# Gate and up projections of a decoder step's feed-forward as seven block products in place of eight, in two passes of 544 tokens

## The reference

```python
def merge_and_ffn(x, conv_out, attn_out, w_out, ffn_norm_g, w_gate, w_up, w_down):
    mix = jnp.concatenate([conv_out, attn_out.astype(conv_out.dtype)], axis=-1)
    x = x + jnp.einsum('bte,ed->btd', mix, w_out)
    h = rms_norm(x, ffn_norm_g)
    f = jax.nn.silu(jnp.einsum('btd,df->btf', h, w_gate)) * jnp.einsum('btd,df->btf', h, w_up)
    return x + jnp.einsum('btf,fd->btd', f, w_down)
```

## Time and profile before

| | us |
|---|---|
| median of 3 runs | 1621.68 |
| lowest, highest run | 1618.64, 1622.87 |
| profiled execution | 1625.65 |
| its span, first to last instruction | 1623.9 |
| PE, DVE, ACT, POOL busy | 1525.2, 888.5, 428.1, 550.8 |
| mean granted PE clock, as a share of 2.4 GHz | 0.973 |

### The profile page before, as it was taken

One profiled execution on the slowest core, in us unless ns is written; L12 is line 12 of the kernel. 1 busy time (PEld: TensorE's weight loads), 2 busy tenths in 40 slices (PEclk: granted clock), 3 DMA queues, 4 the chain that ended last, 5 costly groups with the idle time before them and its releaser, 6 DMA issues.

```text
span 1623.9 us, 24357 instructions
## 1 busy us (share of the span) xinstructions
PE 1525.2 (94%) x9069; PEld 1400.5 (86%) x9069; DVE 888.5 (55%) x1568; ACT 428.1 (26%) x788; POOL 550.8 (34%) x436
## 2 busy tenths in 40 slices
PE   4999988889968888899999999999999999999999
PEld 4998777538846767799989999999999999999999
DVE  7799989999867874444353241423324241433323
ACT  4100258755265554452140101010000101010010
POOL 4543211041258800115333425343342534333320
PEclk9999999989978998899999999999999999999999
DMA  6312100120163331232101101111111111111103
GB/s 209 85 48 73 58 13 25 28 79 7 50 216 118 111 96 42 65 136 80 40 26 52 53 26 55 48 39 50 41 41 37 52 38 52 39 52 39 39 0 110
DMA packets 68638, 100.17 MB, mean 62 GB/s; under 512 B 12017, under 2 KB 49137, under 8 KB 68431
## 3 DMA queue, kind: packets, MB, share of 16 engines
q1 hardware_dynamic: 63714, 94.32, 18.0%
q10 hardware_dynamic: 4853, 4.93, 0.9%
HBM read 86.57 MB, written 13.02 MB: 61 GB/s over the span
## 4 chain that ended last, share of the span: by engine, by line
PE 73%; DVE 13%; issue 6%; ACT 5%; DMA 1%; POOL 1%; ACTq 0%; DVEq 0%; POOLq 0%
PE ps L942 21%; PE ps L944 21%; PE ps L943 21%; DVE mcnt L2193 2%; PE ps L1261 2%; PE ps L1249 1%; ACT rl L1644 1%; PE ps L1233 1%; DVE y L2072 1%; PE ps L1234 1%; PE ps L1346 1%; DVE acc L2134 1%; ACT sm L1791 1%; PE ps L1390 1%; PE ps L1303 1%
## 5 line engine op out<-in xcount | busy, mean ns | idle before, releaser
L942 PE MATMUL ps<-hi_t,w_hi 128*128 128x384 f32 (+2 forms) x1464 | 479.1, 327 | 2.4 <-DVE lo_t L2535 2.4
L944 PE MATMUL ps<-hi_t,w_lo 128*128 128x384 f32 (+2 forms) x1464 | 478.0, 326 | 0.0
L943 PE MATMUL ps<-lo_t,w_hi 128*128 128x384 f32 (+2 forms) x1464 | 477.7, 326 | 0.0
L942 PEld LDWEIGHTS ps<-hi_t,w_hi 128*128 128x128 f32 (+1 forms) x1464 | 274.2, 187 | 3.9 <-issue 1.6
L943 PEld LDWEIGHTS ps<-lo_t,w_hi 128*128 128x128 f32 (+1 forms) x1464 | 274.2, 187 | 0.6
L944 PEld LDWEIGHTS ps<-hi_t,w_lo 128*128 128x128 f32 (+1 forms) x1464 | 274.1, 187 | 0.6
L2599 DVE TENSOR_TENSOR x<-x,ps 128x384 f32<-128x384 f32 (+1 forms) x264 | 139.3, 531 | 105.9 <-PE ps L944 105.2
L942 PE MATMUL ps<-f_hi,w_hi 128*128 128x384 f32 (+1 forms) x528 | 175.4, 332 | 2.9 <-DVE x L2599 2.5
L925 POOL CAST w_hi<-w_raw 128x1024 fp32r<-128x1024 f32 x60 | 62.8, 1047 | 334.8 <-PE ps L944 334.8
L943 PE MATMUL ps<-f_lo,w_hi 128*128 128x384 f32 (+1 forms) x528 | 172.7, 327 | 0.0
L944 PE MATMUL ps<-f_hi,w_lo 128*128 128x384 f32 (+1 forms) x528 | 172.7, 327 | 0.0
(11 more groups left out here) (318 smaller groups left out, 2361.6 us busy)
## 6 DMA issues: line engine op xcount, KB each, us to landing
w_raw<-in_w_gate SPq DMA_DIRECT2D x22, 512.0 KB, 3.5
w_raw<-in_w_up SPq DMA_DIRECT2D x22, 512.0 KB, 3.4
w_raw<-in_w_down SPq DMA_DIRECT2D x22, 512.0 KB, 3.4
w_raw<-in_w_in SPq DMA_DIRECT2D x16, 512.0 KB, 3.6
kt_b<-in_cache_kt SPq DMA_DIRECT2D x48, 128.0 KB, 2.4
v_b<-in_cache_v SPq DMA_DIRECT2D x48, 128.0 KB, 2.4
x<-in_x_t SPq DMA_DIRECT2D x8, 544.0 KB, 7.9
w_raw<-in_w_u SPq DMA_DIRECT2D x8, 512.0 KB, 3.5
```

The source lines that it names most:

```text
L942: pe.matmul(out, a_hi, b_hi, start=first, stop=False)
L943: pe.matmul(out, a_hi, b_lo, start=False, stop=False)
L944: return pe.matmul(out, a_lo, b_hi, start=False, stop=last)
```

## The change

**The product.** Take gate (up is the same). For two F tiles and 544 tokens the weights are a 2x2 block matrix (F tile by half of the 1024 channels) and the inputs another (half of the channels by half of the tokens, 272 each). The product of the two takes eight block products; here it is made of seven (Winograd's form of Strassen's algorithm), for which sums of blocks are formed. On the weights' side these are S1 to S4, on the inputs' side T1 to T4, and the seven results are combined to blocks 11, 12, 21 and 22 of gate (`sum_u2`, `sum_22`, `sum_11`, `sum_21`, `sum_12`). A block product is 4 x 3 matmuls of 272 columns. A pair n (`NPAIR` = 22: 11 groups in each of two passes over half of the tokens) has 7 steps for gate and up each, 14 products, numbered here from 1.

**Inputs.** DVE multiplies x1 by gain and `rs_all` (`normed`), since the sums need finished inputs; the T differences are DVE's, high parts ACT's, low parts DVE's (B11, T1, T2, B22) or POOL's (T3, B21, T4), each of 4 x 272 = 1088 columns. For this the norm's factors are formed by quarters of 272 tokens during the output projection, whose last four tiles are made quarter by quarter (28 outputs in place of 24, on seven banks). The inputs of the second pass are formed in pairs 9 and 10 (`spread` and `switch`).

**Weights.** SP loads halves (256 KB), 12 per pair, in both passes: all weights are read twice. DVE forms S1 to S4 from them in place (`make_s1` to `make_s4`, 512 columns, two SBUF inputs each), ACT the high part of each operand (512 columns; POOL's before), POOL the low part. The 14 operands of a pair go through a ring of seven places. Down's four half operands go the same way.

**Combining.** ACT copies product 1 and 2 out of PSUM (`take_p1`), DVE makes 14 adds of 272 columns from PSUM, silu runs in place on SBUF, then `multiply` (two SBUF inputs), ACT's high part, DVE's low part (`f_low`, two SBUF inputs). POOL no longer scales the silu and DVE no longer scales the gate. Down is 2 x 8 outputs of 272 columns over eight banks; its first half waits for the low part of block 21, its second for that of block 12. DVE adds the 16 outputs to x1. The first half of y is stored between the passes.

The core of the diff, with the parts that the queue orders of a pair are made of:

```diff
-NDOWN = NB * KT
-OUT_ORDER = [(0, 0), (0, 1), (1, 0), (1, 1), (2, 0), (2, 1), (0, 2), (1, 2), (2, 2)]
-OUT_ORDER += [(m, j) for m in range(3, KT) for j in range(NB)]
+HALF, BLK = ROWS // 2, ROWS // 4
+QUARTERS = [(j * BLK, (j + 1) * BLK) for j in range(4)]
+SIDE_BY_SIDE = 4
+OUT_ORDER = [(m, *BLOCKS[j]) for m, j in [(0, 0), (0, 1), (1, 0), (1, 1), (2, 0), (2, 1), (0, 2), (1, 2), (2, 2)]]
+OUT_ORDER += [(3, *BLOCKS[j]) for j in range(NB)]
+OUT_ORDER += [(m, *b) for b in QUARTERS for m in range(SIDE_BY_SIDE, KT)]
+NOUT = len(OUT_ORDER)
...
+PASSES = 2
+NPAIR = PASSES * FG
+NOPS, RING, ND = 14, 7, 4
+PREP = NOPS + ND
+RING_AT = (6, 7, 8, 9, 10, 11, 5)
+DOWN_RAW = 4
+X_BANK, Y_BANK, Z_BANK = (0, 1), (2, 3), (4, 5)
+B11, T1, T2, T3, B21, B22, T4 = range(7)
+STEP_B = (B11, T2, T1, T3, B21, T4, B22)
+STEP_BANK = (X_BANK, Y_BANK, Z_BANK, Y_BANK, X_BANK, Y_BANK, Z_BANK)
...
+SUM22, SUM11, SUM21, SUM12 = range(1, 5)
+def prepared(i):
+    if i < 10:
+        return i + 1
+    return i + 3
...
+            def load_pair(n, row, after, last):
+                if not last:
+                    for mat in range(2):
+                        sp.wait_ge(split_lo, n * PREP + (N_FFN + prepared(6 + mat)))
+                        load_part(mat, 2, after)
+                    for mat in range(2):
+                        sp.wait_ge(s_done, n * 8 + (7 + mat))
+                        load_part(mat, 0, after)
+                sp.wait_ge(split_lo, n * PREP + (N_FFN + down_prepared(1)))
+                load_down(row + P)
+                if not last:
+                    for mat in range(2):
+                        sp.wait_ge(split_lo, n * PREP + (N_FFN + prepared(10 + mat)))
+                        load_part(mat, 3, after)
+                    for mat in range(2):
+                        sp.wait_ge(split_lo, n * PREP + (N_FFN + prepared(12 + mat)))
+                        load_part(mat, 1, after)
+                    sp.wait_ge(split_lo, n * PREP + (N_FFN + PREP))
+                    load_down(after)
...
+            def operand_low(n, i, opening=False):
+                hi, lo = operand(i)
+                src, shaped = operand_source(i, opening)
+                pool.wait_ge(split_hi, n * PREP + (N_FFN + prepared(i)))
+                pool.tensor_tensor(shaped(lo), src, shaped(hi).bitcast(F32), ALU.subtract).then_inc(split_lo, 1)
...
+            def weigh_pair(n, opening, switch, last):
+                for i in range(7, 10):
+                    operand_low(n, i, opening)
+                    if opening and i == 8:
+                        row_inverses(3)
+                for d in range(2):
+                    down_low(n, d)
+                if opening:
+                    b_low(0, T4)
+                for i in range(10, NOPS):
+                    operand_low(n, i, opening)
+                for d in range(2, ND):
+                    down_low(n, d)
+                if last:
+                    return
+                for i in range(7):
+                    operand_low(n + 1, i)
+                    if switch and i == 3:
+                        b_low(1, T3)
+                        b_low(1, B21)
+                if switch:
+                    b_low(1, T4)
...
+            def bank_free(n, opening, step, mat):
+                if opening and step < 3:
+                    bank = STEP_BANK[step][mat]
+                    pe.wait_ge(x1_added, max(s for s in range(NOUT) if s % BANKS_OUT == bank) + 1)
+                elif step == 0:
+                    pe.wait_ge(x1_added, n * 16 + (NOUT - 8))
+                elif step == 1:
+                    pe.wait_ge(x1_added, n * 16 + NOUT)
+                elif step == 3:
+                    pe.wait_ge(comb, n * 14 + (1 + mat))
+                elif step == 4:
+                    pe.wait_ge(p1_left, n * 2 + (1 + mat))
+                elif step == 5:
+                    pe.wait_ge(comb, n * 14 + (3 + 3 * mat))
+                elif step == 6:
+                    pe.wait_ge(comb, n * 14 + (5 + 3 * mat))
+            def product(n, opening, step, mat):
+                i = 2 * step + mat
+                pe.wait_ge(split_lo, n * PREP + (N_FFN + prepared(i)))
+                bank_free(n, opening, step, mat)
+                w_h, w_l = operand(i)
+                x_h, x_l = b_slices(STEP_B[step])
+                for k in range(4):
+                    c = slice(k * P, k * P + P)
+                    mm = three(ps[:, STEP_BANK[step][mat], 0:BLK], w_h[:, c], w_l[:, c], x_h[:, k, :], x_l[:, k, :],
+                               k == 0, k == 3)
+                mm.then_inc(proj_done, 1)
...
+            def feed_pair(n, opening, switch, last):
+                take_p1(n, 0)
+                operand_high(n, 7, opening)
+                take_p1(n, 1)
+                operand_high(n, 8, opening)
+                if switch:
+                    b_high(1, B11)
+                operand_high(n, 9, opening)
+                if opening:
+                    take_scales(3)
+                for d in range(2):
+                    down_high(n, d)
+                if opening:
+                    b_high(0, T4)
+                operand_high(n, 10, opening)
+                operand_high(n, 11, opening)
+                operand_high(n, 12, opening)
+                if switch:
+                    b_high(1, T1)
+                operand_high(n, 13, opening)
+                silu(n, SUM22)
+                f_high(n, SUM22)
+                for d in range(2, ND):
+                    down_high(n, d)
+                silu(n, SUM11)
+                if switch:
+                    b_high(1, T2)
+                if not last:
+                    operand_high(n + 1, 0)
+                f_high(n, SUM11)
+                if not last:
+                    operand_high(n + 1, 1)
+                silu(n, SUM21)
+                f_high(n, SUM21)
+                if not last:
+                    operand_high(n + 1, 2)
+                    operand_high(n + 1, 3)
+                if switch:
+                    b_high(1, T3)
+                    b_high(1, B21)
+                silu(n, SUM12)
+                f_high(n, SUM12)
+                if switch:
+                    b_high(1, B22)
+                if not last:
+                    operand_high(n + 1, 4)
+                    operand_high(n + 1, 5)
+                    operand_high(n + 1, 6)
+                if switch:
+                    b_high(1, T4)
...
+            def sum_22(n, mat):
+                dve.wait_ge(proj_done, n * NOPS + (BASE[5] + (7 + mat)))
+                dve.wait_ge(comb, n * 14 + (1 + mat))
+                dve.tensor_tensor(u3_sum(mat), ps[:, Y_BANK[mat], 0:BLK], u2_sum(mat), ALU.add).then_inc(comb, 1)
+                dve.wait_ge(comb, n * 14 + (3 + 3 * mat))
+                dve.tensor_tensor((gate_sum, up_sum)[mat](SUM22), ps[:, Z_BANK[mat], 0:BLK], u3_sum(mat), ALU.add
+                                  ).then_inc(comb, 1)
+                dve.tensor_tensor(u2_sum(mat), ps[:, Z_BANK[mat], 0:BLK], u2_sum(mat), ALU.add).then_inc(comb, 1)
...
+            def combine_pair(n, h, opening, spread, switch, last):
+                if opening:
+                    row_variances(3)
+                    b_low(0, B22)
+                sum_u2(n, 0)
+                sum_u2(n, 1)
+                if opening:
+                    row_diagonals(3)
+                    make_t4(0)
+                if spread:
+                    normed(1, 0, 0)
+                if switch:
+                    b_low(1, B11)
+                    make_t1(1)
+                make_s4(n, 0)
+                make_s4(n, 1)
+                sum_22(n, 0)
+                sum_22(n, 1)
+                if switch:
+                    b_low(1, T1)
+                multiply(n, SUM22)
+                sum_11(n, 0)
+                sum_11(n, 1)
+                f_low(n, SUM22)
+                multiply(n, SUM11)
+                if switch:
+                    make_t2(1)
+                f_low(n, SUM11)
+                if spread:
+                    normed(1, 1, 0)
+                if not last:
+                    make_s1(n + 1, 0)
+                sum_21(n, 0)
+                if not last:
+                    make_s1(n + 1, 1)
+                sum_21(n, 1)
+                if not last:
+                    make_s3(n + 1, 0)
+                multiply(n, SUM21)
+                if not last:
+                    make_s3(n + 1, 1)
+                f_low(n, SUM21)
+                if not last:
+                    make_s2(n + 1, 0)
+                    make_s2(n + 1, 1)
+                if switch:
+                    b_low(1, T2)
+                    make_t3(1)
+                sum_12(n, 0)
+                sum_12(n, 1)
+                multiply(n, SUM12)
+                add_down(n, h, 0)
+                add_down(n, h, 1)
+                f_low(n, SUM12)
+                for q in range(2, 16):
+                    add_down(n, h, q)
+                    if spread and q == 7:
```

(15 more changed lines are left out.)

645 lines of the change are left out of this document (420 added, 225 removed).

## The result

The changed kernel takes **1709.56 us** (median of 4 runs, 1707.54 to 1713.67) against 1621.63 for the kernel before (4 runs, 1618.64 to 1622.87): a ratio of 1.0548, interval 1.0524 to 1.0573. It is 87.9 us slower, where 57.7 were forecast. The profiled execution's span is 1711.9 us, for 1623.9.

The account below looks back on a forecast made before the run. PE's matmul start rate was taken to bound the 801.9 us feed-forward. 22 pairs of 38.3 us, + 16 for opening and switch, + 1.0, make 859.6: +57.7, so 1679 us; range 1636 to 1722, faster 0.27, same 0.05, slower 0.68.

Parts of the forecast that it names:

- Matmul price: Feed-forward matmuls on PE: 126 ns for each matmul of 272 columns, so 33.3 us per pair and 732 us for 22 pairs.
- The lock: DVE instructions with two SBUF inputs wait for POOL's current instruction, and POOL's next waits in turn; 16 such per pair.
- The walk: One pair followed step by step: low part 21 ends at 24.9 us, down starts at 25.0, PE stalls 3.9 us.
- Without any lock the same chain: Lower bound in a pair: DVE's chain behind product 10 ends near 23.0 us even without waits for POOL, stall 1.8.
- The period: Time T of one pair: 33.3 + 3.9 + 0.4 = 37.5 us with rounding, plus 0.8 clock loss (0 to 1.6), 38.3.
- The 0.4 for the fifth output's bank: In each pair's down part, the fifth output waits for a bank behind DVE's first down add: 0.4 us more.
- Opening: Pair 0: POOL's input splits and weight parts make operand 10 some 9 us late; +8 us (3 to 14).
- 8 us of normed inputs, partly in its free time, and 10 us of splits and differences in one pair: +8 (3 to 14): Switch before pass two: DVE's work for the second pass's inputs adds 8 us to the kernel.
- Norm sums and scales by quarter hide between outputs: Output projection in 16 quarters: 95.9 us for 94.9, +1.0; the fourth quarter's norm work costs a few small matmuls.
- PE is nearly fed: Rival, chance 0.27: DVE gets past POOL between product 22 and low part 21; T = 35.1, kernel 1603 us.
- The clock falls twice as long: Rival, chance 0.11: the clock falls at every stall for two half-speed stretches; T = 40.7, kernel 1732 us.
- Loads become the wait: Rival, chance 0.05: late down halves add 3 us per pair, T = 41.3, 1746 us; the forecast itself took transfers at 0.

## Why the prediction was right in kind and short in size

- **Matmul price, right.** 126 ns at 272 columns was taken and measured. The 116 ns estimated by the Trainium skill's rule (TensorE: Matmul & The Clock Gate, Part 1) do not hold in this loop.
- **The lock, right.** Low parts near 1 us and 512-column sums above it are there, and the runs without POOL's work and with an operand in PSUM show it to be the cause in this order of the queues. POOL over 60% busy was foretold too: 197.86 of 308.9 us, 64%.
- **The walk, right to 0.2 us at its end, in part by luck.** Low part 21 was put at 24.9 and came at 24.7, with a stall of 3.5 us for 3.9. On the way low part 11 ended at 19.8 and the first weight sum at 21.5, each 0.6 us later than in the walk. The second weight sum, which the walk had held by POOL until 22.1, ran free in 0.67 us, since POOL was out of work at 21.0. The two errors cancel.
- **"Without any lock the same chain (5.8 us of DVE work behind product 10, two ACT steps between) ends near 23.0, a stall of 1.8": wrong.** It ends by 21.2, and the stall is 0.1. The step added durations where DVE's starts are closer, and let ACT's steps stand in line where one of them runs beside DVE. It was a bound of the range and the price of the first rival (T = 35.1). Measured without the lock, a pair takes 33.6, so the lock costs 5 us per pair and not 3.2.
- **The period, short by 0.4 us, 10 us in all.** 38.3 was forecast and 38.6 to 38.9 measured. The mis-sized term is the clock: 0.8 was taken, and filling the wait gives 1.35 back (inside 0 to 1.6). The 0.4 for the fifth output's bank is not there beside it, as the lower clock covers it: for both, 1.2 was taken and 1.75 measured. Against that, down begins 0.2 us earlier than forecast.
- **Opening, mis-sized.** +8 (3 to 14) was taken; pair 0 costs 13.1 over a steady pair. By the stretch view 5.2 of them are more idle time of PE (8.7 us for 3.5 in a steady pair) and 7.9 are more busy time (43.1 us for 35.1) at a clock of 0.82 for 0.94. The term had only late operands in it and nothing for the clock. The operands it named, behind POOL's splits, are not what PE waited for: its waits were for DVE's diagonal (3.4 us), which waited for POOL, and for DVE's low part (5.3).
- **"8 us of normed inputs, partly in its free time, and 10 us of splits and differences in one pair: +8 (3 to 14)": the largest miss.** It cost 20.2, outside the bounds. PE's idle time in pairs 9 to 11 is 28.9 us, 18.5 more than in three steady pairs, with a wait of up to 10.7 us. These are DVE and POOL instructions with SBUF inputs on both sides, put in large part ahead of low part 21; the free time that the term counted on stands elsewhere in the pair. Two runs bear this out: with POOL's weight parts thin the three pairs take 113.9 us, and with the same work moved behind low part 21 and over more pairs 116.3. With the 4.9 us that the last pair gives back, opening and switch stand at 28.4 net for 16: 12 us.
- **"Norm sums and scales by quarter hide between outputs": wrong.** +1.0 was taken for the output projection, and that was right for its quarters (0.9; by its own 165.2 ns the term has 95.2 and not 94.9 us before). But PE spends 3.9 us on the norm's small matmuls ahead of the first product and waits 2.3 ahead of the last six of them; with smaller gaps it is 7.6 us in all. With 1.8 us further up, which are not the change's, the feed-forward begins 9.3 us later: 8 us above the forecast.

The sum of the misses, 10 + 12 + 8, is the 30 us between 57.7 and 87.9. The direction does not hang on the two large misses: 22 steady pairs alone, 851.4 us, are longer than the 801.9 of before.

**Rivals.** "PE is nearly fed" is not so here, but it is what two edits of order and operands make of the kernel. "The clock falls twice as long" holds in part: the clock fell in every steady pair, and in six of the 17 it stayed low twice as long as in the others; these take 39.4 to 39.7 us, the others 38.2 to 38.5. "Loads become the wait" is not so in the steady pairs. In pair 11 it is: ACT waited 2.4 us for down halves and down started 2.1 us later than in a steady pair, which is a part of the switch's 20.2. So the price of zero for transfers was too low there, and in three profiles of reordered versions one pair each (pair 1 or 19) took 4.0 to 5.5 us more behind such a load.

## What to carry to other kernels

A trade of matmuls for vector work must be costed on the order in which the side engines work, not on their shares. Here VectorE and GpSimd each had a third of the time free, and the kernel became 5.5% slower by who waits for whom. Where VectorE and GpSimd both run from SBUF, count VectorE's instructions with two SBUF inputs on PE's path, and give each an operand in PSUM or put it where nobody waits. One-off work put into a loop must be walked through in its place like the rest. The pairs that hold it here take 132 to 136 us with the period at 38.7, 34.5 or 33.2 us, so it costs 20 us in the late loop and 33 in the other two.

## What the runs showed of the hardware beyond the forecast

- VectorE's fp32 instructions start closer than they last: 0.35 us apart at 0.43 us for 272 columns, 0.60 at 0.68 for 512 (run without POOL's work).
- PE idled 3.5 us in each steady pair of the changed kernel and the granted clock fell in each, which costs 1.35 us per pair. With 27 filling matmuls in that place it stayed at 1.00, and the kernel was 26 us shorter, if still 3.7% slower than before.
- GpSimd's 512-column subtracts with nothing to hold them take 1.28 us (1.29 was worked out from 320, 384 and 1024 columns) and up to 2.34 in the line shown when held: the hold works in both directions.
